# How far ahead of TensorE the order list puts VectorE's and ScalarE's expert slots

## The chip, the core and the metric

The kernel runs on one core of a Trainium2 chip. The metric is the device time of one launch in microseconds (us). TensorE, VectorE, ScalarE, GpSimd (POOL in the rows) and SyncE (SP) each run their own instruction stream and meet through semaphores.

## What is computed

Two layers of a diffusion backbone over 256 context tokens and 256 latent tokens of width 1024, all in float32: attention of two kinds behind one input projection, an output projection, and a feed-forward part that retrieves experts. The last of these is where the change acts:

```python
def peer_ffn(h, p):                       # per block of 128 tokens
    q = (xb @ p['peer_wq']).reshape(128, 8 heads, 2, 128)
    s = einsum('thcd,ckd->thck', q, subkeys);  sv, si = top_k(s, 16)
    cand = all 16 x 16 sums of the two halves;  top_s, pos = top_k(cand, 16)
    eidx = expert number of each;  gate = softmax(top_s)          # 8 x 16 = 128 experts a token
    u, v = peer_u[eidx], peer_v[eidx]                              # rows of 1024 each
    act = gelu(einsum('ted,td->te', u, xb)) * gate
    return einsum('te,ted->td', act, v)
for l in range(2):
    x, xc = x + g1 * attention(x, xc), ...;  x = x + g2 * peer_ffn(norm(x));  (the same for xc in layer 0)
```

Layer 0 has four blocks of 128 tokens in this part (two of context, two latent), layer 1 has two. So there are 6 blocks of 128 expert slots each, 768 slots.

## The kernel before

**A slot** is one expert for each of a block's 128 tokens. GpSimd gathers its u and v rows from HBM into one of eight buffers of EXPERT (L628, 128 partitions x 2048 floats, about 1 MB). VectorE takes the dot product of u with the token (L1524, into DOT; CUSTOM in the trace, ISA in the order's rows). ScalarE makes the Gelu of it (L1107, GEL), times the gate (L1109, WEI), and for three slots of four a diagonal matrix of the weights (L1114, DIAG, three buffers). TensorE multiplies that diagonal by v into two PSUM banks VS (L924, two products that the profile shows as four matmul records). Every fourth slot goes to VectorE instead (L1534, ACC), after the dot of the slot behind it. A buffer of EXPERT comes free when TensorE, or for a fourth slot VectorE, has used it; the gather of the slot eight further on waits for that (L620, L628). ScalarE can write a DIAG buffer only when TensorE has used the one three TensorE slots back.

**The background** is everything else: projections ("in", "up", "out": TensorE L784, L812, weights of 0.25 to 0.5 MB a piece by SyncE), transposes (L716), attention ("attn", one stage a head: scores L852, row maximum on VectorE L1355, exponential on ScalarE L1055, transposes, product with V L860), and the choosing of experts ("pick" and "more", for a second tile of tokens "also" and "then": key queries on TensorE L914, scores L895, top-16 on VectorE L1463 to L1491, then the expert numbers L1496 to L1517).

**Order.** PLAN is one list of stages, made by hand-written rules when the program is built. It lays background stages and slots in one row, mostly one or two slots behind each stage where background is plentiful, four or five where it is not. TensorE and SyncE go through PLAN as it stands. VectorE and ScalarE go through `late(PLAN)`, in which a slot may stand ahead of background that TensorE does first. In the kernel before, of each run of consecutive slots only the first is moved ahead, over the stages directly before it, up to a summed cost of LEAD = 130 (the costs are VectorE's share of a stage by the table COST: 45 for "pick", 40 for "more", 35 for "attn", 40 for an "in" of two tiles). `put_off` says whether a stage may be passed: not a "close", and not the stage that picks the experts of the slot itself or of the next 16. GpSimd gathers in the order of slots.

```python
LEAD = 130                                     # before
while run > 0 and jumped < LEAD and put_off(out[at - 1], first):
    at, run, jumped = at - 1, run - 1, jumped + cost(out[at - 1])
```

Of the kernel before, what the change touches and what calls it, by code (L numbers as in the profile page):

```python
# [30 lines left out]
SLOTS = PH * TOPK  # L31
# [15 lines left out]
AHEAD = 16  # L47
# [18 lines left out]
def blocks_of(l, g):  # L66

    return [4 * l + 2 * g - (2 if l else 0) + t for t in range(2)]
# [83 lines left out]
def mingle(first, second):  # L152
# [4 lines left out]
    for n, s in enumerate(first):  # L157
# [12 lines left out]
COST = {"stat": (45, 0), "norm": (50, 0), "in": (0, 20), "turn": (0, 10), "root": (5, 5), "up": (0, 25), "attn": (35, 0),  # L170
        "hnorm": (20, 0), "heads": (20, 0), "gates": (10, 0), "out": (0, 22), "back": (20, 0), "pick": (45, 0), "more": (40, 0), "also": (45, 0), "then": (40, 0),
        "ada": (18, 0), "adae": (4, 0), "adat": (10, 0), "mod": (5, 0)}
# [3 lines left out]
def cost(s):  # L176
    each, per_tile = COST[s[0]]
    return each + per_tile * (len(s[PER_TILE[s[0]]]) if s[0] in PER_TILE else 0)


def picks_of(stage):

    if stage[0] not in ("more", "then") or stage[3] == 0:
        return []
    _, l, g, h, ts = stage
    return [blocks_of(l, g)[ts[0]] * SLOTS + TOPK * (h - 1)]
# [53 lines left out]
def spans(plan):  # L240

    out = []
    for s in plan:
        if s[0] == "slots" and out and out[-1][0] == "slots" and out[-1][1] == s[1] and out[-1][3] == s[2]:
            out[-1] = ("slots", s[1], out[-1][2], s[3])
        else:
            out.append(s)
    return out
# [41 lines left out]
PLAN = make_plan()  # L290


LEAD = 130


def put_off(stage, slots):

    return stage[0] in COST and not any(at <= slots[1] * SLOTS + slots[3] - 1 + AHEAD for at in picks_of(stage))


def late(plan):

    out, run = [], 0
    for s in plan:
        if s[0] == "slots":
            _, b, q0, q1 = s
            first, at, jumped = ("slots", b, q0, q0 + 1), len(out), 0  # L310
            while run > 0 and jumped < LEAD and put_off(out[at - 1], first):
                at, run, jumped = at - 1, run - 1, jumped + cost(out[at - 1])
            if at == len(out):
                out.append(s)
            else:
                out.insert(at, first)
                out += [("slots", b, q0 + 1, q1)] if q1 > q0 + 1 else []
            run = 0
        else:
            out.append(s)  # L320
            run += 1
    at = {s: n for n, s in enumerate(out)}
    for s in out:
        if s[0] == "slots":
            need = s[1] * SLOTS + (s[3] - 1) // TOPK * TOPK
            assert any(at[p] < at[s] for p in out if need in picks_of(p)), "slots before their pick"
    return out
# [77 lines left out]
def backbone(nc, a, out):  # L405
    ctx = ExitStack()
    with ctx:
# [548 lines left out]
        def _(act):  # L956
# [180 lines left out]
            for stage in late(PLAN):  # L1137
                if stage[0] in do:
                    do[stage[0]](stage)

        @block.vector
        def _(dve):
# [449 lines left out]
            for stage in late(PLAN):  # L1592
                if stage[0] in do:
                    do[stage[0]](stage)
# [43 lines left out]
```

## Time and profile before

| | |
|---|---|
| median of three runs | 2957.7 us (2955.98 to 2963.01) |
| the profiled execution | 2969.66 us, span of its records 2967.8 us |
| busy in the span | TensorE 2190.0, VectorE 1854.1, ScalarE 1148.0, GpSimd 969.0 us |
| mean granted TensorE clock | 0.877 |
| HBM traffic | 973.56 MB read, 328 GB/s over the span |

Slots run from about 259 us to the end, with a break from about 2000 to 2161 us, where layer 0 has none left and layer 1 none chosen yet. Windows of the trace give busy times and the DMA engines' share by stretch; the views of waits say who waited for whom; the timeline shows single instructions. A wait is idle time of an engine that ended with the event named behind the arrow.

### The profile page before, as it was taken

The numbers are of one execution on the slowest core, as the hardware profiler recorded it, in microseconds if no ns is written. First come the engines' busy times: TensorE is split into PE (matmuls) and PEld (weight loads), VectorE is DVE, ScalarE is ACT, GpSimd is POOL, SyncE is SP. The second block draws the span as 40 slices with busy tenths as digits, with TensorE's granted clock in tenths as the row PEclk, the third lists the DMA queues.
The fourth block names the chain that finished last, engine by engine and source line by source line (L and its number), as shares of the span: only waits on it lengthen the run. The fifth ranks groups of instructions, "written<-read, shape, count | busy, mean of one in ns | idle before, by whom it ended". The sixth has DMA issues, their size and how long they took to land.

```text
span 2967.8 us, 26078 instructions
## 1 busy us (share of the span) xinstructions
PE 2190.0 (74%) x6768; PEld 1104.7 (37%) x6768; DVE 1854.1 (62%) x4482; ACT 1148.0 (39%) x3024; POOL 969.0 (33%) x916
## 2 busy tenths in 40 slices
PE   5997677658777787777767877868766777766765
PEld 2544334433433334333323323324533333433322
DVE  0136765874457656888876565543487565777775
ACT  2123463452246725434453243331234454343432
POOL 1012223223223233434443444430033323344553
PEclk9988788879899898888888999988877989889988
DMA  8478879878787698889999999994298969999997
GB/s 296 137 266 312 301 272 347 307 282 333 296 317 252 250 331 328 330 349 398 420 421 372 410 419 416 416 412 145 93 368 318 374 229 356 340 389 416 414 417 309
DMA packets 210714, 976.18 MB, mean 329 GB/s; under 512 B 17533, under 2 KB 70297, under 8 KB 112281
## 3 DMA queue, kind: packets, MB, share of 16 engines
q0 software_dynamic: 123648, 855.69, 73.1%
q1 hardware_dynamic: 86936, 118.99, 11.7%
q8 instruction: 55, 0.90, 0.1%
q14 instruction: 75, 0.61, 0.1%
HBM read 973.56 MB, written 1.05 MB: 328 GB/s over the span
## 4 chain that ended last, share of the span: by engine, by line
PE 40%; DVE 20%; DMA 16%; ACT 15%; issue 7%; POOL 1%; SPq 0%; POOLq 0%; DVEq 0%; ACTq 0%
PE VS L924 19%; DMA EXPERT<-in_peer_uv,FIX 15%; PE PA L784 8%; DVE EXPERT L1524 5%; ACT L1107 3%; PE PB L914 3%; ACT DIAG L1114 2%; DVE SCR L1159 2%; ACT WEI L1109 2%; PE PA L812 2%; PE PB L852 2%; DVE ACC L1534 1%; ACT SCR L1055 1%; ACT GEL L1107 1%; PE VS L742 1%
## 5 line engine op out<-in xcount | busy, mean ns | idle before, releaser
L924 PE MATMUL VS<-EXPERT,DIAG 128*128 128x512 f32 x2304 | 1294.0, 701 | 629.2 <-ACT DIAG L1114 628.3
L628 POOL DMA_INDIRECT EXPERT<-in_peer_uv,FIX x768 | 899.9, 1172 | 1396.4 <-PE VS L924 837.6
L1524 DVE CUSTOM_DVE_ANT_0 EXPERT<-EXPERT,H 128x1024 f32<-128x1024 f32 x768 | 920.8, 1223 | 245.7 <-DMA EXPERT<-in_peer_uv,FIX 234.8
L924 PEld LDWEIGHTS VS<-EXPERT,DIAG 128*128 128x128 f32 x2304 | 469.2, 218 | 1292.2 <-ACT DIAG L1114 835.0
L1107 ACT ACTIVATE GEL<-DOT 128x1 f32<-128x1 f32 x768 | 154.9, 202 | 1093.4 <-DVE DOT L1524 1082.2
L784 PE MATMUL PA<-WT,HT 128*128 128x512 f32 (+2 forms) x768 | 322.9, 567 | 12.2 <-ACT HT L1011 6.0
L1534 DVE SCALAR_TENSOR_TENSOR ACC<-EXPERT,WEI,ACC 128x1024 f32<-128x1024 f32 x192 | 246.2, 1282 | 52.8 <-ACT WEI L1109 52.2
L1114 ACT ACTIVATE DIAG<-IDN,WEI 128x128 f32<-128x128 f32 x576 | 231.2, 401 | 44.8 <-PE VS L924 26.3
L1109 ACT ACTIVATE WEI<-GEL,GATE 128x1 f32<-128x1 f32 x768 | 226.3, 295 | 25.0
L784 PEld LDWEIGHTS PA<-WT,HT 128*128 128x128 f32 x768 | 150.2, 198 | 173.9 <-issue 143.8
L914 PEld LDWEIGHTS PB<-HT,WT 128*128 128x128 f32 x1280 | 188.1, 211 | 33.0 <-issue 26.9
L914 PE MATMUL PB<-HT,WT 128*128 128x128 f32 (+1 forms) x1280 | 198.7, 314 | 1.6 <-issue 1.6
L1107 ACT ACT_TABLE_LOAD x115 | 147.5, 1283 | 6.0
L1355 DVE TENSOR_REDUCE MX<-PB 128x1 f32<-128x512 f32 (+1 forms) x96 | 55.5, 598 | 125.5 <-PE PB L852 125.4
L654 POOL DMA_DIRECT2D EXPERT<-in_w_ada x48 | 34.5, 720 | 292.4 <-PE VS L742 270.5
L620 POOL COPY FIX<-IDX 128x8 uint32 (+1 forms) x96 | 34.4, 359 | 277.7 <-PE VS L924 160.1
L1091 ACT COPY SCR<-PB 128x128 f32<-128x128 f32 (+1 forms) x80 | 22.6, 283 | 195.6 <-PE PB L914 193.6
L1055 ACT ACT_TABLE_LOAD x50 | 64.2, 1283 | 63.2 <-PE PB L852 62.7
L1055 ACT ACTIVATE SCR<-PB,NM 128x512 f32<-128x512 f32 (+1 forms) x96 | 58.7, 614 | 75.1 <-DVE NM L1372 74.3
L1463 DVE MAX8 SV<-PA 128x8 f32<-128x128 f32 x96 | 23.7, 288 | 99.8 <-PE PA L895 99.7
L716 PE MATMUL PB<-IDN,SCR 128*128 128x128 f32 (+1 forms) x374 | 55.3, 294 | 23.9 <-DVE SCR L1159 9.3
L716 PEld LDWEIGHTS PB<-IDN,SCR 128*128 128x128 f32 (+1 forms) x374 | 47.2, 149 | 55.9 <-issue 20.1
(141 smaller groups left out, 1753.8 us busy)
## 6 DMA issues: line engine op xcount, KB each, us to landing
EXPERT<-in_w_ada POOLq DMA_DIRECT2D x48, 1024.0 KB, 11.2
WT<-in_peer_wq SPq DMA_DIRECT2D x80, 512.0 KB
WT<-in_w_in SPq DMA_DIRECT2D x56, 512.0 KB
WT<-in_w_out SPq DMA_DIRECT2D x40, 512.0 KB
EXPERT<-in_peer_uv,FIX POOLq DMA_INDIRECT x768
WT<-in_w_in SPq DMA_DIRECT2D x16, 384.0 KB
WT<-in_w_in SPq DMA_DIRECT2D x20, 288.0 KB
WT<-in_mla_wk_up SPq DMA_DIRECT2D x5, 512.0 KB
```

Source lines behind the costliest of these rows:

```text
L628: pool.indirect_dma_start(out=EXPERT[:, j, :], out_offset=None, in_=a["peer_uv"], in_offset=bass.IndirectOffsetOnAxis(ap=FIX[:, par, j:j + ...
L716: last = nc.tensor.transpose(bank[0:rows, i * P:(i + 1) * P], s, IDN[:, :])
L784: last = nc.tensor.matmul(bank[:, 0:n], HT[:, k, t * P:(t + 1) * P], w[:, k % KP, 0:n], start=(k == 0), stop=(k == KD - 1))
L812: last = nc.tensor.matmul(bank[:, 0:n], HT[:, k0 + k, t * P:(t + 1) * P], w[:, k % KP, 0:n], start=(k == 0), stop=(k == kn - 1))
L914: last = nc.tensor.matmul(bank[:, mine], held["w"][k // HP][:, k % HP, c * P:(c + 1) * P], HT[:, k, mine], start=(k == 0), stop=(k == KD - 1))
L924: ins = nc.tensor.matmul(VSUM[n][:, :], DIAG[:, i, :], EXPERT[:, j, D + n * W:D + (n + 1) * W], start=first, stop=last_one)
L1055: ins = nc.scalar.activation(PR[:, h % 2, c, 0:keys], bank[:, 0:keys], ACT.Exp, bias=NM[:, h % 2, c:c + 1], scale=SC_M if h < MH else SC_D ...
L1107: nc.scalar.activation(GEL[:, one], DOT[:, j:j + 1], ACT.Gelu).then_inc(gelu_ready, 1)
L1109: nc.scalar.activation(WEI[:, one], GEL[:, one], ACT.Copy, scale=gate).then_inc(wei_ready, 1)
L1114: nc.scalar.activation(DIAG[:, i, :], IDN[:, :], ACT.Copy, scale=WEI[:, one]).then_inc(diag_ready, 1)
L1524: nc.vector.tensor_tensor_reduce(out=EXPERT[:, j, 0:D], in0=EXPERT[:, j, 0:D], in1=H2[:, b % HB, :], scale=1.0, scalar=0.0, op0=ALU.mult, ...
L1534: nc.vector.scalar_tensor_tensor(out=ACC[:, :], in0=EXPERT[:, j, D:2 * D], scalar=WEI[:, BY_PE:BY_PE + 1], in1=ACC[:, :], op0=ALU.mult, op ...
```

## The change

Only the list of VectorE and ScalarE changes. TensorE's rows, SyncE's and GpSimd's are the same as before, instruction for instruction; lines move up by one number. Now every slot is moved, not the first of a run alone. A slot passes stages until it meets another slot, a stage that `put_off` keeps, a summed cost of LEAD = 70, or a stage that TensorE reaches more than LEAD_SLOTS = 3 slots earlier. Since slots that were moved leave the stages behind them, the next slot can pass them again.

```diff
-LEAD = 130
-def put_off(stage, slots):
-    return stage[0] in COST and not any(at <= slots[1] * SLOTS + slots[3] - 1 + AHEAD for at in picks_of(stage))
+LEAD = 70
+LEAD_SLOTS = 3
+def put_off(stage, slot):
+    return stage[0] in COST and not any(at <= slot[1] * SLOTS + slot[2] + AHEAD for at in picks_of(stage))
 def late(plan):
-    out, run = [], 0
+    out, before, no = [], {}, 0
     for s in plan:
...
+        if s[0] != "slots":
             out.append(s)
-            run += 1
+            before[s] = no
+            continue
+        for i in range(s[2], s[3]):
+            slot, at, jumped = ("slots", s[1], i, i + 1), len(out), 0
+            while (at > 0 and out[at - 1][0] != "slots" and put_off(out[at - 1], slot) and jumped < LEAD
+                   and no - before[out[at - 1]] <= LEAD_SLOTS):
+                at, jumped = at - 1, jumped + cost(out[at - 1])
+            out.insert(at, slot)
+            no += 1
+    out = spans(out)
```

Counted on the two lists: before, 303 of the 768 slots stand ahead of TensorE's order, nearly all by one stage; now 635 do, 254 by one stage, 316 by two, 65 by three to five. No slot stands later than before.

VectorE while the experts of the second context tile are chosen (head 2): before, between the end of a "pick" (L1491) and the start of its "more" (L1496) stand the dots of slots 73 and 74.

```order
L1491 MAX_INDEX POS<-TS,SCR 128x8
L1524 ISA EXPERT,DOT<-EXPERT,H 128x1024
L1524 ISA DOT 128x1
L1524 ISA EXPERT,DOT<-EXPERT,H 128x1024
L1524 ISA DOT 128x1
L1496 TENSOR_SCALAR AB<-POS 128x16
```

The same place now:

```order
L1490 MAX_INDEX POS<-TS,SCR 128x8
L1523 ISA EXPERT,DOT<-EXPERT,H 128x1024
L1523 ISA DOT 128x1
L1533 SCALAR_TENSOR_TENSOR ACC<-EXPERT,WEI,ACC 128x1024
L1523 ISA EXPERT,DOT<-EXPERT,H 128x1024
L1523 ISA DOT 128x1
L1495 TENSOR_SCALAR AB<-POS 128x16
```

Now these are the dots of slots 76 and 77 (the row into ACC, the fourth-slot product of slot 75, always follows the dot of 76): three slots later ones stand at the same stage.

ScalarE in attention of the first latent tile, between the exponential of the last head with one map and that of the first with two (x2). Before, slots 160 and 161:

```order
L1055 ACTIVATE SCR,SUM<-PB,NM 128x512
L1107 ACT_TABLE_LOAD
L1107 ACTIVATE GEL<-DOT 128x1
L1109 ACTIVATE WEI<-GEL,GATE 128x1
L1114 ACTIVATE DIAG<-IDN,WEI 128x128
L1107 ACTIVATE GEL<-DOT 128x1
L1109 ACTIVATE WEI<-GEL,GATE 128x1
L1114 ACTIVATE DIAG<-IDN,WEI 128x128
L1055 ACT_TABLE_LOAD
L1055 ACTIVATE SCR,SUM<-PB,NM 128x512 x2
```

Now, slots 162 and 163:

```order
L1054 ACTIVATE SCR,SUM<-PB,NM 128x512
L1106 ACT_TABLE_LOAD
L1106 ACTIVATE GEL<-DOT 128x1
L1108 ACTIVATE WEI<-GEL,GATE 128x1
L1113 ACTIVATE DIAG<-IDN,WEI 128x128
L1106 ACTIVATE GEL<-DOT 128x1
L1108 ACTIVATE WEI<-GEL,GATE 128x1
L1054 ACT_TABLE_LOAD
L1054 ACTIVATE SCR,SUM<-PB,NM 128x512 x2
```

Slot 163, a fourth one, has no DIAG. Two slots stand there as before, but two numbers further on. The count of table loads in ScalarE's list is 193 in both programs.

VectorE at the input projection of the latent tiles (the key chunk, whose rotation L1159 waits for the end of TensorE's products). Before, the slot directly ahead of it is 113, followed by 114:

```order
L1524 ISA EXPERT,DOT<-EXPERT,H 128x1024
L1524 ISA DOT 128x1
L1159 TENSOR_TENSOR SCR<-PA,ROPD 128x256 x2
L1159 TENSOR_TENSOR SCR<-PA,ROPD 128x512
L1159 TENSOR_TENSOR SCR<-SCR 128x512
```

Now it is 116:

```order
L1523 ISA EXPERT,DOT<-EXPERT,H 128x1024
L1523 ISA DOT 128x1
L1533 SCALAR_TENSOR_TENSOR ACC<-EXPERT,WEI,ACC 128x1024
L1158 TENSOR_TENSOR SCR<-PA,ROPD 128x256 x2
L1158 TENSOR_TENSOR SCR<-PA,ROPD 128x512
L1158 TENSOR_TENSOR SCR<-SCR 128x512
```

Three more slots are through VectorE when it reaches the rotation. TensorE does slots 113 and 114 behind the products that the rotation waits for.

## Rows read from the trace of the kernel before

**Rows 1.** The page: chain that ended last; the groups of the slot's matmul and dot.

```profile
PE VS L924 19%; DMA EXPERT<-in_peer_uv,FIX 15%; PE PA L784 8%; DVE EXPERT L1524 5%; ACT L1107 3%; PE PB L914 3%; ACT DIAG L1114 2%; DVE SCR L1159 2%; ACT WEI L1109 2%; PE PA L812 2%; PE PB L852 2%; DVE ACC L1534 1%; ACT SCR L1055 1%; ACT GEL L1107 1%; PE VS L742 1%
...
L924 PE MATMUL VS<-EXPERT,DIAG 128*128 128x512 f32 x2304 | 1294.0, 701 | 629.2 <-ACT DIAG L1114 628.3
...
L1524 DVE CUSTOM_DVE_ANT_0 EXPERT<-EXPERT,H 128x1024 f32<-128x1024 f32 x768 | 920.8, 1223 | 245.7 <-DMA EXPERT<-in_peer_uv,FIX 234.8
```

**Rows 2.** Windows: from:to, length, busy time by engine, clock, DMA share, GB/s.

```profile
core 0: us, PE busy (x) PEld busy (x) DVE busy (x) ACT busy (x) POOL busy (x), PEclk, DMA share, GB/s
259.00:1269.00 1010.00, 749.73 (x2334) 393.49 (x2334) 673.95 (x1726) 457.02 (x1099) 305.37 (x290) 0.87 0.83 309
1269.00:2000.00 731.00, 550.18 (x1331) 244.28 (x1332) 497.11 (x1054) 279.35 (x829) 321.03 (x294) 0.90 0.99 403
2161.00:2613.00 452.00, 326.79 (x1003) 165.87 (x1003) 304.59 (x755) 198.69 (x504) 150.44 (x145) 0.86 0.87 334
2613.00:2968.00 355.00, 232.63 (x564) 101.93 (x564) 246.86 (x509) 125.45 (x389) 154.95 (x137) 0.86 0.95 387
503.00:640.00 137.00, 94.00 (x385) 58.27 (x383) 110.07 (x392) 52.62 (x136) 37.09 (x36) 0.83 0.83 314
534.15:550.32 16.17, 11.12 (x48) 7.02 (x48) 13.89 (x50) 6.58 (x17) 5.23 (x5) 0.87 0.83 310
640.00:860.00 220.00, 171.72 (x437) 82.08 (x436) 107.77 (x194) 69.32 (x202) 62.38 (x61) 0.90 0.82 308
860.00:1040.00 180.00, 137.99 (x504) 70.90 (x502) 126.86 (x256) 126.03 (x244) 53.50 (x50) 0.91 0.72 264
```

**Rows 3.** TensorE's waits (total, times, longest), the first four windows in order.

```profile
PE VS L924 <- ACT DIAG L1114: 236.3, 95, 6.8
...
PE VS L924 <- ACT DIAG L1114: 166.9, 87, 5.4
...
PE VS L924 <- ACT DIAG L1114: 120.2, 45, 7.9
...
PE VS L924 <- ACT DIAG L1114: 104.9, 49, 9.4
```

**Rows 4.** The same for windows 503:640 (choosing), 640:860 (projections), 860:1040 (attention).

```profile
PE VS L924 <- ACT DIAG L1114: 42.6, 11, 6.8
...
PE VS L924 <- ACT DIAG L1114: 40.5, 15, 5.2
...
PE VS L924 <- ACT DIAG L1114: 38.9, 24, 5.3
```

**Rows 5.** VectorE's waits: two in 259:1269, one in 860:1040, one in 1269:2000.

```profile
DVE SCR L1159 <- PE PA L784: 75.2, 8, 17.8
...
DVE EXPERT L1524 <- DMA EXPERT<-in_peer_uv,FIX: 2.5, 4, 1.2
...
DVE MX L1355 <- PE PB L852: 40.2, 13, 7.1
...
DVE EXPERT L1524 <- DMA EXPERT<-in_peer_uv,FIX: 142.0, 107, 3.1
```

**Rows 6.** Timeline: start, duration, instruction [idle before it <-releaser].

```profile
529.79 1.88 PE L924 MATMUL VS<-EXPERT,DIAG 128*128 128x512 f32 x4
...
535.28 3.33 PE L924 MATMUL VS<-EXPERT,DIAG 128*128 128x512 f32 x4 [3.61 <-ACT DIAG L1114]
...
541.05 1.28 ACT L1107 ACT_TABLE_LOAD   x1
542.35 0.20 ACT L1107 ACTIVATE GEL<-DOT 128x1 f32<-128x1 f32 x1
...
551.46 3.78 PE L924 MATMUL VS<-EXPERT,DIAG 128*128 128x512 f32 x4 [5.06 <-ACT DIAG L1114]
...
725.62 2.53 PE L924 MATMUL VS<-EXPERT,DIAG 128*128 128x512 f32 x4 [3.58 <-ACT DIAG L1114]
...
914.60 3.68 PE L924 MATMUL VS<-EXPERT,DIAG 128*128 128x512 f32 x4 [4.16 <-ACT DIAG L1114]
```

More of the change, by code:

```diff
@@ L290 @@
 PLAN = make_plan()
-LEAD = 130
-def put_off(stage, slots):
-    return stage[0] in COST and not any(at <= slots[1] * SLOTS + slots[3] - 1 + AHEAD for at in picks_of(stage))
+LEAD = 70
+LEAD_SLOTS = 3
+def put_off(stage, slot):
+    return stage[0] in COST and not any(at <= slot[1] * SLOTS + slot[2] + AHEAD for at in picks_of(stage))
 def late(plan):
-    out, run = [], 0
+    out, before, no = [], {}, 0
     for s in plan:
[L308 to L319, printed above, removed]
-            out.append(s)
-            run += 1
+        if s[0] != "slots":
+            out.append(s)
+            before[s] = no
[8 more added lines that the diff above has]
+    out = spans(out)
     at = {s: n for n, s in enumerate(out)}
```

## The prediction, written before the changed kernel ran

> **What bounds the kernel now.** I read the page first. No engine is full, TensorE being busy 2190 of 2968 us, and one wait stands out: the slot's matmuls waited 628.3 us for the diagonal that ScalarE makes for them, 21% of the span [rows 1]. The chain that ended last runs through these matmuls (19%) and through the gathers (15%) in about equal parts, so the limit changes with the place. The windows say where [rows 2]. From 1269 to 2000 us and from 2613 us to the end the DMA engines' share is 0.99 and 0.95, at 403 and 387 GB/s: 1086 us in which the gathers set the pace. From 259 to 1269 and from 2161 to 2613 us the share is 0.83 and 0.87: 1462 us in which something else does. The waits for DIAG divide into 236.3 + 120.2 = 356.5 us in the second kind and 166.9 + 104.9 = 271.8 us in the first [rows 3], together the 628.3.
>
> In the DMA-bound stretches VectorE stands 142.0 us in 107 waits for gathers that have not landed, from 1269 to 2000 us alone. From 259 to 1269 us it waits so for 2.5 us in all [rows 5]. There the data is in place, and what is late is the dot on VectorE, since a background stage is ahead of it. The timeline shows the pattern [rows 6]: the slot at 529.79 us, first of its run and so moved ahead before, starts without a wait and takes 1.88 us. The slots at 535.28 and 551.46 us wait 3.61 and 5.06 us, each for a dot that VectorE did only after a whole top-16; 725.62 us is the same behind a rotation, 914.60 us the same in attention. Here the wait changes sides: VectorE in its turn waits for TensorE's stages, 75.2 us for projections (L784) from 259 to 1269 us, and 40.2 us for scores in the attention window alone, about what TensorE waits for DIAG there, 38.9 us [rows 4, 5]. Two engines in turn, neither full. That is time a longer lead can overlap.
>
> After a long wait TensorE also runs slower: the four records take 1.88 us where none came before, 3.33 and 3.78 us behind waits of 3.61 and 5.06 us [rows 6], the mark of the 1.2 GHz level against 2.4. The granted clock is 0.83 to 0.91 in the latency-bound windows [rows 2]. A wait that goes gives back up to 1.5 to 1.9 us more.
>
> **The change, part by part.** It adds and removes no instruction. It moves dots (L1524), fourth-slot products (L1534) and ScalarE's GEL, WEI and DIAG ahead of background on their two engines; no DMA is issued there. So the cost side is delay of what is passed, the gain side the waits above. It also lowers LEAD from 130 to 70; since no slot ends up later than before, that costs nothing against the old order.
>
> *Choosing experts, all stretches of it outside the DMA-bound time:* 259 to 365, 503 to 640, 1148 to 1269, 2161 to 2300 and 2510 to 2613 us, 606 us together (borders read off the timeline, an estimate to some us). One head from 534.15 to 550.32 us takes 16.17 us, of which VectorE is busy 13.89 [rows 2]. With any lead a head can't be shorter than that: at most 2.28 us go. The gathers allow it, 0.83 x 16.17 = 13.4 us. VectorE will still wait a little for the scores and for WEI, so I take half, 1.14 of 16.17 us or 7.05%: 606 x 0.0705 = 43 us. Ends: 0, if VectorE meets the same waits elsewhere, and 85.
>
> *Attention,* 365 to 450, 860 to 1040, 2345 to 2440 us, 360 us: in the middle window TensorE waits 38.9 of 180 us for DIAG, with VectorE busy 127, ScalarE 126, TensorE 138 [rows 2, 4]. A stage there needs all three engines one after the other (scores, maximum, exponential, transposes), and the stage that is passed feeds TensorE's next. I take a third of the wait, 13.0 us in 180, so 26 us in 360. Ends: 0 and two thirds, 52.
>
> *Projections and what lies around them,* 450 to 503, 640 to 860, 1040 to 1148, 2440 to 2510 us, 451 us: in 640 to 860 us the wait is 40.5 of 220 us, VectorE is busy only 108 [rows 2, 4]. Again a third, 13.5 in 220, so 451 / 220 x 13.5 = 28 us. There is more idle time on VectorE here, but the DMA share of 0.82 leaves only 0.18 x 220 = 40 us before the gathers and weights fill it, and ScalarE can't be more than three DIAG buffers ahead whatever the list says. Ends: 0 and 55.
>
> All three together, 97 us, lie well under what the DMA engines would allow: 0.17 x 1010 + 0.13 x 452 = 230 us [rows 2].
>
> *The DMA-bound stretches,* 1086 us: four or five slots stand between two stages, and a dot moved ahead starts no earlier than its gather lands. TensorE's 271.8 us of waits stay under other names or the same. I take 0. Ends: a gain of 0.01 x 731 + 0.05 x 355 = 25 us from the share that is left, and a loss of as much: a stage now stands behind up to three dots that each wait 142.0 / 107 = 1.3 us for a landing, which the slots that TensorE does in between (1.88 us each) hide; if that cover were gone in every sixth of about 100 stages there, it would cost 17 times 1.3, or 22 us.
>
> *Late stages elsewhere:* where nothing waits for a landing, a stage is later by the dots that passed it, 1.22 us each [rows 1], while TensorE has one or two slots of 1.88 us to do. I cost this at nothing beyond the halves and thirds taken above.
>
> *A rule on ScalarE's tables.* The rows show a table load of 1.28 us at 541.05 us, and the Gelu behind it starts at 542.35 us, 0.02 us after its end [rows 6]; the count of loads is 193 in either program. The Trainium skill ("ScalarE: Activation LUTs", What ACT_TABLE_LOAD costs) states a drain of about 1.38 us beside each load, some 2.66 us a switch. With that, ScalarE's 126 us in the attention window would be near full and the attention term 0, the time 26 us longer; by the trace the drain isn't there.
>
> **Sum.** 43 + 26 + 28 = 97 us off the profiled execution's 2969.7 us gives 2873. The median of the runs lies 12 us under that execution, so the forecast for the median is **2861 us**.
>
> **Rivals.** *The wait changes its name.* TensorE no longer waits at L924 but at the next stage, for the maximum, transposed copy or key query that is now behind more dots. For it: the two engines hand stages to each other in attention. Against: outside L924 TensorE waits hardly at all now, so there is slack. It would leave a quarter of the gain, 24 us: 2934 us.
>
> *ScalarE binds in attention.* It is busy 126 of 180 us there, and its DIAG now waits for TensorE's slot three back with the exponential queued behind. Then that term is 0: 2887 us.
>
> *Slower: the ring.* Two blocks, 256 slots, take the 1010 us of the first window, so the eight buffers make one trip in 8 x 1010 / 256 = 32 us; the next 256 take 731 us, a trip in 23 us with the queue full. Some 9 us are thus to spare, and dots three slots ahead use up about 3 x 3.9 = 12 us. If VectorE now meets unlanded gathers in the first kind too, it stands there with the stage behind it, and TensorE runs dry. About 230 stages lie in these stretches; at 1.3 us each it decides from 97 / 1.3 = 75 of them, a third. If half are hit, 115 x 1.3 = 150 us are lost against 97 won: 3011 us. Against it: 2.5 us of landing waits now.
>
> *The change does nothing:* the three DIAG buffers and VectorE's own queue keep the real lead where it is. 2958 us.
>
> **Chances.** Forecast 0.60; wait renamed 0.17, of which a tenth ends inside the bound; ScalarE 0.08; ring 0.10; nothing 0.05. A change of 0.3% (9 us) is about what a measurement of this kernel can tell from none. Faster 0.60 + 0.08 + 0.15 = 0.83, within 0.3% 0.07, slower 0.10. The range reaches down to most of the upper ends, about 160 us of the 85 + 52 + 55 = 192: 2795 us, and up past the renamed wait to 2948 us.
>
> **What would show it.** Right: the DIAG wait falls from 356.5 to 200 us or less in the latency-bound stretches, the DMA share there rises to about 0.9, the DMA-bound stretches keep their length within 25 us, and the heads of the choosing take about 15 us. VectorE's 75.2 us at L784 grow shorter or are met by full DIAG buffers. Wrong: new TensorE waits at L860, L716, L784 or L895 of tens of us (renamed wait), landing waits of VectorE far above 2.5 us in the first stretch (ring), or ScalarE near full in attention.

## The result, and the profile after

The changed kernel takes 2759.9 us (2755.77 to 2763.04, four runs) where the kernel before takes 2960.4 us: ratio 0.9322, 95% interval 0.9301 to 0.9343, 200 us less. The forecast was 2861 us with a range of 2795 to 2948. The direction was right, the gain forecast (97 us) was half of the one measured, and the time lies below the range. The two profiled executions, 2969.7 and 2755.8 us, are 214 us apart; readings from the traces add up to that and not to 200.

The page of the changed kernel: span, busy time, chain that ended last, and the groups of slot matmul and dot that answer to [rows 1].

```profile
span 2753.9 us, 26076 instructions
...
PE 2117.5 (77%) x6768; PEld 1091.8 (40%) x6768; DVE 1852.2 (67%) x4482; ACT 1145.8 (42%) x3024; POOL 970.6 (35%) x916
...
DMA EXPERT<-in_peer_uv,FIX 21%; PE VS L923 12%; PE PA L783 9%; DVE EXPERT L1523 7%; DVE ACC L1533 2%; PE PA L811 2%; DVE SCR L1158 2%; PE PB L913 2%; ACT L1106 1%; PE VS L741 1%; ACT L1054 1%; ACT WEI L1108 1%; PE PB L851 1%; ACT HT L1010 1%; ACT DIAG L1113 1%
...
L923 PE MATMUL VS<-EXPERT,DIAG 128*128 128x512 f32 x2304 | 1197.6, 662 | 310.5 <-ACT DIAG L1113 309.6
...
L1523 DVE CUSTOM_DVE_ANT_0 EXPERT<-EXPERT,H 128x1024 f32<-128x1024 f32 x768 | 925.6, 1224 | 353.9 <-DMA EXPERT<-in_peer_uv,FIX 344.1
```

The wait for DIAG is halved, 628.3 to 309.6 us. What the same matmuls are busy fell too, from 1294.0 to 1197.6 us, although there are as many and of the same size. That second number turned out to matter.

Windows of the changed kernel (from:to, length, busy time by engine, clock, DMA share, GB/s). The first four are cut at the dots of slots 0, 256, 512 and 640. The last three hold the same matmuls as 503:640, 640:860 and 860:1040 of [rows 2], to within one record:

```profile
261.00:1124.00 863.00, 702.51 (x2334) 382.74 (x2334) 671.34 (x1725) 455.97 (x1099) 308.62 (x289) 0.92 0.94 361
1124.00:2016.00 892.00, 674.77 (x1903) 328.19 (x1903) 561.19 (x1248) 313.51 (x908) 325.42 (x302) 0.87 0.88 354
2016.00:2414.00 398.00, 307.31 (x1019) 166.23 (x1019) 311.48 (x766) 201.65 (x509) 152.46 (x146) 0.88 0.98 394
2414.00:2754.00 340.00, 230.28 (x548) 99.30 (x548) 240.36 (x499) 121.08 (x384) 153.98 (x135) 0.88 0.95 388
472.00:583.60 111.60, 85.52 (x385) 58.05 (x383) 106.71 (x378) 48.40 (x129) 38.77 (x37) 0.89 0.99 384
583.60:776.10 192.50, 165.60 (x436) 80.71 (x437) 114.17 (x210) 73.90 (x210) 63.92 (x60) 0.92 0.89 344
776.10:923.50 147.40, 130.65 (x505) 70.54 (x504) 122.37 (x252) 124.53 (x239) 55.95 (x51) 0.97 0.88 334
```

The first latency-bound stretch (slots 0 to 256; a stretch where the engines wait for each other and not for gathers) went from 1010 to 863 us, TensorE's busy time in it from 749.7 to 702.5 us and its clock from 0.87 to 0.92. The second, from slot 512 to slot 640, went from 465 us (2161 to 2626) to 398. Slots 256 to 512 with the break behind them took 892 us before (1269 to 2161) and take 892 now; the last stretch 342 and 340. So 147 + 67 us came from the latency-bound stretches, and all the rest is as it was.

What TensorE waits for in the first stretch, then what VectorE does (total, times, longest):

```profile
PE VS L923 <- ACT DIAG L1113: 50.4, 21, 7.1
PE PA L894 <- ACT SCR L1090: 36.8, 11, 4.6
PE PA L859 <- DVE SCR L1368: 12.6, 14, 1.9
...
DVE EXPERT L1523 <- DMA EXPERT<-in_peer_uv,FIX: 37.1, 28, 2.8
DVE SCR L1158 <- PE PA L783: 31.9, 8, 8.1
```

DIAG's 236.3 us [rows 3] are 50.4. Some waiting has other names now, of which the two largest make 49 us, so that TensorE's idle time in the stretch fell by 100 us (260.3 to 160.5) where the wait for DIAG fell by 186. VectorE waits 37.1 us for landings where it waited 2.5 [rows 5]. Both rivals are to be seen; the halved gathers below say what the second cost.

### The profile page after: what moved, and what is told of

Read it like the earlier page. It is cut to its first block, busy times and chain, and to the rows that moved or that the text cites. A ratio compares the mean times of both kernels' runs of the same rounds, so it can differ in the third digit from the quotient of the medians.

```text
span 2753.9 us, 26076 instructions
## 1 busy us (share of the span) xinstructions
PE 2117.5 (77%) x6768; PEld 1091.8 (40%) x6768; DVE 1852.2 (67%) x4482; ACT 1145.8 (42%) x3024; POOL 970.6 (35%) x916
## 4 chain that ended last, share of the span: by engine, by line
PE 33%; DVE 23%; DMA 23%; ACT 12%; issue 7%; POOL 1%; POOLq 0%; SPq 0%; DVEq 0%; ACTq 0%
DMA EXPERT<-in_peer_uv,FIX 21%; PE VS L923 12%; PE PA L783 9%; DVE EXPERT L1523 7%; DVE ACC L1533 2%; PE PA L811 2%; DVE SCR L1158 2%; PE PB L913 2%; ACT L1106 1%; PE VS L741 1%; ACT L1054 1%; ACT WEI L1108 1%; PE PB L851 1%; ACT HT L1010 1%; ACT DIAG L1113 1%
## 5 line engine op out<-in xcount | busy, mean ns | idle before, releaser
L923 PE MATMUL VS<-EXPERT,DIAG 128*128 128x512 f32 x2304 | 1197.6, 662 | 310.5 <-ACT DIAG L1113 309.6
L923 PEld LDWEIGHTS VS<-EXPERT,DIAG 128*128 128x128 f32 x2304 | 462.9, 212 | 912.0 <-issue 469.7
L913 PE MATMUL PB<-HT,WT 128*128 128x128 f32 (+1 forms) x1280 | 204.4, 320 | 15.7 <-issue 15.7
L1106 ACT ACT_TABLE_LOAD x115 | 147.5, 1283 | 6.6 <-ACT SCR L1054 0.8
L715 PE MATMUL PB<-IDN,SCR 128*128 128x128 f32 (+1 forms) x374 | 55.9, 295 | 73.2 <-DVE SCR L1307 21.5
L715 PEld LDWEIGHTS PB<-IDN,SCR 128*128 128x128 f32 (+1 forms) x374 | 45.1, 145 | 104.6 <-ACT SCR L999 26.3
L894 PE MATMUL PA<-SKT,SCR 128*128 128x128 f32 x192 | 38.4, 342 | 60.0 <-ACT SCR L1090 60.0
L811 PE MATMUL PA<-WT,HT 128*128 128x512 f32 (+1 forms) x136 | 65.9, 636 | 17.5 <-ACT HT L1042 10.1
L894 PEld LDWEIGHTS PA<-SKT,SCR 128*128 128x128 f32 x192 | 33.0, 239 | 84.7 <-ACT SCR L1090 75.1
```

The source lines that it names most:

```text
L715: last = nc.tensor.transpose(bank[0:rows, i * P:(i + 1) * P], s, IDN[:, :])
L811: last = nc.tensor.matmul(bank[:, 0:n], HT[:, k0 + k, t * P:(t + 1) * P], w[:, k % KP, 0:n], start=(k == 0), stop=(k == kn - 1))
L913: last = nc.tensor.matmul(bank[:, mine], held["w"][k // HP][:, k % HP, c * P:(c + 1) * P], HT[:, k, mine], start=(k == 0), stop=(k == KD - 1))
L923: ins = nc.tensor.matmul(VSUM[n][:, :], DIAG[:, i, :], EXPERT[:, j, D + n * W:D + (n + 1) * W], start=first, stop=last_one)
L1106: nc.scalar.activation(GEL[:, one], DOT[:, j:j + 1], ACT.Gelu).then_inc(gelu_ready, 1)
```

## The experiments

### One stage, or several?

`one_stage` lets every slot pass one stage and no more; `pair` does so only for the first two slots behind a stage; `slots1` and `slots2` narrow the distance (how many slots earlier TensorE may reach the stage) and keep LEAD = 70; `lead130` lets a slot pass more stages.

```diff
 one_stage:  LEAD = 1,   LEAD_SLOTS = 3
 pair:       LEAD = 1,   LEAD_SLOTS = 1
 slots1:     LEAD = 70,  LEAD_SLOTS = 1
 slots2:     LEAD = 70,  LEAD_SLOTS = 2
 lead130:    LEAD = 130, LEAD_SLOTS = 3
```

> The new rule with LEAD = 1: every slot may pass exactly one stage, never two; 635 of 768 slots stand one stage ahead (before: 303, after: 635, of which 381 by two or more). Theory A (the wait sits at the second slot of each run of two, which the old rule left behind its stage; passing that one stage ends it): at least two thirds of the 200 us come, 2825 us or less. Theory B (one stage of VectorE's work, up to 5 us of top-16, is longer than one slot of TensorE, so the second stage of lead is needed): less than half comes, 2860 to 2930 us.

> LEAD = 1 and LEAD_SLOTS = 1: only the first two slots behind a stage stand ahead of it, by that one stage. Against the old rule, 206 slots are moved, all of them second slots but a few, each by one stage, and some first slots lose a second stage. Theory A (second slots): this smallest edit brings 170 us or more, 2790 us or less. Rival (a standing lead that carries over from stage to stage is needed): 2830 us or more.

> LEAD_SLOTS = 1 instead of 3, LEAD 70 kept: a slot may pass a stage only if TensorE reaches it at most one slot earlier; 509 slots ahead instead of 635. Theory A (second slots): most of the gain, near 2800 us, since second slots still pass their stage. Theory B (depth): well under half, 2870 to 2930 us.

> LEAD_SLOTS = 2: 579 slots ahead. Theory A: within 15 us of the changed kernel (2760). Theory B: a clear step between one and three, 2790 to 2830 us.

> The new rule with LEAD = 130 instead of 70: 121 slots pass three stages and 219 two (70: 34 and 316). If the latency-bound stretches are now full by the gathers (DMA share 0.94 and 0.98 there), nothing is left to win: 2750 to 2765 us. If depth still pays, 2740 or less. If stages that are passed too far make TensorE wait (the renamed wait), 2775 us or more.

| kernel | us | ratio to before (95%) |
|---|---|---|
| pair | 2760.2 | 0.9318 (0.9288 to 0.9347) |
| one_stage | 2761.8 | 0.9321 (0.9306 to 0.9337) |
| slots1 | 2759.1 | 0.9324 (0.9298 to 0.9350) |
| slots2 | 2746.0 | 0.9271 (0.9256 to 0.9287) |
| the change | 2759.9 | 0.9322 (0.9301 to 0.9343) |
| lead130 | 2779.0 | 0.9370 (0.9343 to 0.9397) |

Theory A holds and B falls. `pair` moves 206 slots more than the old rule, by one stage, and brings the whole 200 us. Counted on the two lists, all 206 are second slots of their run. The depth beyond one stage adds nothing to the total. The old rule moved the first slot of each run, and in a run of two the second stayed behind the stage, so TensorE met the full length of VectorE's stage once a run. [rows 6] shows the pair: the slot at 529.79 us without a wait, the next, at 535.28 us, with 3.61.

By stretch the depth is not nothing. Slots 0 to 256 in `pair`:

```profile
258.00:1139.00 881.00, 704.59 (x2336) 380.25 (x2334) 672.64 (x1726) 456.68 (x1099) 303.26 (x290) 0.92 0.93 354
```

One stage brings 129 of the 147 us there, and the change 18 us more. It loses them further on: from slot 256 to 512 `pair` takes 881 us and the change 892, from 512 to 640 they take 395 and 398. These are single profiled executions, and `slots2` and `slots2_warm` (below), which have the same program from slot 256 to 512, differ by 6 us there. So the 18 us look real, and where they are lost is less sure.

More depth still even costs: every run of `lead130` is slower than every run of the change, by 19 us in the median. Three of TensorE's waits over the whole of `lead130` (total, times, longest):

```profile
PE VS L923 <- ACT DIAG L1113: 306.7, 142, 9.4
PE PA L894 <- ACT SCR L1090: 59.6, 22, 6.3
...
PE PB L715 <- DVE SCR L1307: 23.8, 6, 8.0
```

and over the whole of `one_stage`:

```profile
PE VS L923 <- ACT DIAG L1113: 463.5, 251, 9.4
PE PA L799 <- DVE GD L1158: 27.8, 14, 3.4
...
PE PA L894 <- ACT SCR L1090: 14.2, 8, 3.8
```

One stage of lead leaves 157 us more of DIAG waits than `lead130` has, and is 17 us faster. Part of what the deep leads no longer wait for DIAG they wait at L894 and L715: the renamed wait of the forecast is real. A total of one named wait is no measure of the kernel. But it does not explain why `lead130` is slower than the change, which waits as long at L894 over the whole:

```profile
PE PA L894 <- ACT SCR L1090: 60.0, 23, 4.6
```

The 19 us are lost between slots 0 and 256 (882.5 us against 863.2). There TensorE's waits for DIAG and at L894 and L859 add up to 94 us in `lead130` and 100 us in the change, and VectorE's wait for landings grew from 37.1 us to this:

```profile
DVE EXPERT L1523 <- DMA EXPERT<-in_peer_uv,FIX: 54.5, 35, 5.4
```

That speaks for the ring rather than for the renamed wait; no run separates the two. LEAD_SLOTS = 2 is the best of the six, 14 us under the change in the median, with an interval clear of the change's.

### Where

The new rule for blocks 0, 1 and 4 alone (`new_where_late`), or for 2, 3 and 5 alone (`new_where_dma`), the other slots by the old rule:

```diff
+        slow = s[1] in (0, 1, 4)
+        if not slow:          # new_where_dma: if slow
+            (the old rule: the first slot of the run, LEAD = 130)
+            continue
         for i in range(s[2], s[3]):
```

> The new rule for the slots of blocks 0, 1 and 4 alone (the latency-bound stretches); the slots of blocks 2, 3 and 5 stand as before. Theory: all of the gain is made there and the rest is bound by the gathers, so 2755 to 2770 us. Rival (the gain is also in the DMA-bound stretches, or is paid for there): 2790 us or more, or under 2745.

> The opposite: the new rule for blocks 2, 3 and 5 alone. Theory: no change, 2950 to 2970 us (before: 2960). Rival: 20 us or more off it either way.

Measured: 2753.6 us, ratio 0.9297 (0.9263 to 0.9330), a little under the 2755 to 2770 expected, and 2966.7 us, ratio 1.0021 (1.0008 to 1.0034). All of the gain is made in the latency-bound blocks. In the gather-bound ones the new order is worth nothing and may cost 0.2%. `slots2_late` put the two best readings together:

> LEAD_SLOTS = 2 and only for the latency-bound blocks 0, 1 and 4, the rest as before: the two best readings put together. If both were real: 2735 to 2750 us, under the changed kernel's 2760 by 10 or more. If they were noise between placements: 2745 to 2765.

2750.3 us, ratio 0.9272 (0.9246 to 0.9299): no better than `slots2`, and a time that both expectations allow. Differences below 10 us are not resolved.

### Do the gathers bound it now?

The DMA share in the shortened stretches is 0.94 to 0.98. Both kernels were run with gathers of half the bytes, from a table of the u rows alone. The v half of each buffer keeps what was there, so these kernels leave the experts' v rows out of the result; two runs each:

```diff
-    out=EXPERT[:, j, :], ... in_=a["peer_uv"]
+    out=EXPERT[:, j, 0:D], ... in_=a["peer_uv"]       # u rows alone
```

> The kernel before, with gathers of the u rows alone (half the bytes; the v half of each buffer keeps what was there, so the weighted sums are left without their experts' values). Theory C (in the old order the latency-bound 1462 us are set by VectorE and TensorE in turn, not by the gathers): they keep 95% of their length, and only the 1086 DMA-bound us shrink, to what the engines need. Rival: everywhere shorter in the same proportion.

> The same halved gathers in the changed kernel. Theory D (with the change the gathers have become the bound of the former latency-bound stretches too, DMA share 0.94 and 0.98): those two, 863 and 387 us long, get at least 8% shorter, so that the change is worth more here than 200 us. Rival E (they are bound by VectorE and TensorE and the high DMA share is only a company): they shorten by under 3%.

Windows of `half_before`, slots 0 to 256, and of `half_after`, slots 0 to 256 and 512 to 640:

```profile
261.00:1270.00 1009.00, 748.62 (x2334) 392.38 (x2334) 672.91 (x1725) 457.02 (x1099) 305.34 (x289) 0.87 0.55 173
```

```profile
256.00:1115.00 859.00, 703.78 (x2334) 385.15 (x2334) 669.63 (x1725) 454.81 (x1099) 310.76 (x289) 0.92 0.63 204
1882.00:2257.00 375.00, 299.86 (x1022) 161.19 (x1021) 309.98 (x767) 201.29 (x509) 154.35 (x147) 0.91 0.70 231
```

`half_before` takes 2803.1 us and keeps 1009 us in the first stretch: theory C holds. `half_after` takes 2524.1 us, but its first stretch keeps 859 of 863 us at a DMA share of 0.63, and the second 375 of 398. Theory D falls for the first: a share of 0.94 was company and no bound, and its landing waits of 37.1 us, the mark of the ring rival, cost it no more than those 4 us. The second, at 0.98, got 6% shorter, between what the two theories had said: there some 23 us hang on the bytes gathered, and VectorE's landing waits of 37.9 us fall to 5.3. Cut at the same matmuls in both traces, it is the choosing of experts that gets shorter (524 to 495 us over both stretches); projections keep their 387 and 386 us and attention its 293 and 297. What the halving saves otherwise is in the DMA-bound blocks.

### The clock that a wait takes with it

TensorE's books: before, the span of 2967.8 us was 2190.0 busy and 777.8 idle; after, 2117.5 busy and 636.4 idle. Of 214 us, 141 are idle time and 73 are busy time of the same work at a higher clock. To price the second part without touching the order, small matmuls of a zero block were put ahead of slots, in the kernel before: twelve ahead of each of 92 second slots in `warm`, whether they waited or not, eight ahead of slots that had waited 2.4 us or more in the others. They add zeros to the slot sum. The edit of the others:

```diff
+    if kind == "one" and slot_no(b, v0) in WARM_AT:
+        for n in range(WARM):
+            nc.tensor.matmul(VSUM[0][0:32, 0:P], ZERO[:, :], IDN[:, :], start=False, stop=False)
```

> The kernel before, with 12 matmuls of a zero block (32 columns of zeros times the 128-wide identity, added into the slot sum, about 1.5 us in all) ahead of the wait of 92 second slots in blocks 0, 1 and 4. Nothing of the order changes; TensorE is merely busy in a part of its wait. Theory (a wait costs its own length and then a stretch of matmuls at 1.2 GHz, and this second part is what the sum left out): the slot matmuls' busy time falls by 40 us or more, the time by 20 to 60 us. Rival (the clock plays no part): busy time of the slots unchanged, time the same or up to 30 us longer.

> The kernel before, with 8 of the zero matmuls (1.2 to 1.9 us by the 263 us that 1104 of them took in the run warm) ahead of the 65 slots that waited 2.4 us or more in the latency-bound stretches, 254.9 us together; so they should fit inside the waits and cost nothing themselves. Those slots' matmuls took 3.4 us each on the mean, 1.5 more than at 2.4 GHz. Theory (the clock after a wait is itself on the path): up to 65 x 1.5 = 98 us of slot time come back and 30 to 90 us of the total, 2870 to 2930 us. Rival (a slot's own matmuls after a wait are not what the next stage waits for, the gain comes from the order alone): slot time falls, the total stays within 10 us of 2960.

> The kernel before, with the same 8 zero matmuls ahead of the 48 slots that waited 2.4 us or more in the DMA-bound stretches (168.5 us of waits, their matmuls 3.1 us each on the mean, so up to 60 us of slot time to be had). Theory (there the gathers set the pace, and neither order nor clock of TensorE matters): total within 9 us of 2961. Rival (the clock is on the path everywhere): 20 to 40 us less.

`warm` gave 2965.9 us, ratio 1.0008 (0.9995 to 1.0020), with the slots' busy time 66 us down, to 1228.3: the busy time fell as its theory expected, the time did not. Taken alone it says that the clock is not on the path. But its 1104 zero matmuls took 263.2 us, 2.9 us for each slot instead of the 1.5 expected, and in the trace of before 49 of the 92 slots had waited less than that, 27 of them less than 1 us. So it is inconclusive.

`warm_long`, with eight zero matmuls (128.5 us in 65 places, 2.0 us each) where the wait is 2.4 us or more, gave 2904.9 us, ratio 0.9810 (0.9794 to 0.9827): 57 us less with no instruction of the old order moved. Its slot group with the waits:

```profile
L927 PE MATMUL VS<-EXPERT,DIAG 128*128 128x512 f32 x2304 | 1234.9, 673 | 518.4 <-ACT DIAG L1120 518.1
```

The slots' busy time is 59 us down, nearly all of it at the 65 slots (220.8 to 162.1 us), and the total 57. The wait for DIAG is 110 us shorter because the zero matmuls fill it. The first stretch is 979 us instead of 1010 (dot of slot 0 at 259.3 us, of slot 256 at 1238.2). `warm_dma` took 42 us off the slots' busy time in the gather-bound blocks, to 1252.5, and 4 us off the total: 2957.3 us, ratio 0.9988 (0.9977 to 1.0000). So the clock is on the path where TensorE and VectorE hand work to each other, and off it where gathers set the pace.

Does it come on top of the new order?

> The new rule with LEAD_SLOTS = 2 and the 8 zero matmuls ahead of the 11 latency-bound slots that still wait 2.4 us or more there (50.9 us, matmuls of 3.7 us on the mean). Theory (the new order has already collected the clock's share, since its waits are gone): at most 11 x 1.8 = 20 us less than slots2, 2726 to 2746 us. Rival (clock and order are separate gains, so that the 57 us of warm_long come on top): 2700 us or less.

2744.8 us, ratio 0.9264 (0.9247 to 0.9281), against 2746.0 for `slots2`. Hardly anything comes on top: the waits that it would have to fill are gone. The eleven slots that were left took 40.2 us in `slots2` and take 31.3, so 9 us were to be had, too little to be told from none in the total.

## Why the forecast was wrong

**Where the gain lies: right.** The division into latency-bound and DMA-bound stretches, 0 for the latter, held to 2 us, and `new_where_dma` confirms it. So did the reading of the slots in [rows 6] as two engines in turn. That the gathers leave room for the gain held for the first stretch; in the second, at a DMA share of 0.98, halving them gave back some 23 us. Of the 230 us that the forecast said the DMA engines would allow, 214 were used.

**The three terms: each mis-sized, by the same two steps.** Since TensorE's list is the same, both traces can be cut at the same matmuls, those at the borders that the forecast used, and each row below is the same work. Idle and busy are TensorE's, in us, each figure rounded by itself:

| | before | after | gain | from idle | from busy | in the sum (upper end) |
|---|---|---|---|---|---|---|
| choosing experts | 605 | 524 | 81 | 47 | 35 | 43 (85) |
| attention | 363 | 293 | 71 | 56 | 15 | 26 (52) |
| projections | 447 | 387 | 61 | 41 | 20 | 28 (55) |
| together | 1416 | 1203 | 212 | 143 | 69 | 97 (192) |

The first step that failed is "I take half" and "I take a third". Nothing in the trace supported a half or a third; it was caution put into a term. In the middle window of choosing VectorE is now busy 106.7 of 111.6 us, 96%, and seven heads in a row take 13.4 us each where they took 16.5: VectorE's own busy time became the bound there, as the ceiling of 13.89 in 16.17 us had said, and the discount below that ceiling was wrong. In attention the wait for DIAG went from 38.9 us [rows 4] to this, in 776.1 to 923.5 us:

```profile
PE VS L923 <- ACT DIAG L1113: 1.0, 3, 0.3
```

with new waits of TensorE of 8.6 us at L859 the largest. Against 87.9 us of DIAG waits in all attention before, TensorE's idle time fell by 56, two thirds and not one; against 86.5 us in projections by 41, about half. Had the shares been right, the idle part alone would have been 143 us instead of 97.

The second step is the clock. The forecast noted that "A wait that goes gives back up to 1.5 to 1.9 us more" and then left it out of the sum, and out of the bounds. It is the 69 us of the column "from busy": the same matmuls in less time, in attention 138.0 us before and 130.9 now, at a clock of 0.97 in that window instead of 0.91 [rows 2]. It alone takes projections past their upper end; attention had passed its own by idle time, and choosing stayed inside. `warm_long` prices the clock at 57 us by itself (it did not reach every slot: 21 of the 65 still took over 3 us, where 55 had, and the one at 539.82 us took 3.78 us after 3.19 us more of waiting). With 97 + 69 = 166 us the forecast would have been 2792 us; the shares make the other 46 us.

```profile
534.70 1.93 PE L936 MATMUL VS<-IDN,ZERO 128*32 128x128 f32 x16
539.82 3.78 PE L927 MATMUL VS<-EXPERT,DIAG 128*128 128x512 f32 x4 [3.19 <-ACT DIAG L1120]
```

**The range.** Its lower end took "most of the upper ends" of terms whose ends lacked the clock. The sum of those ends, 192 us, is still 8 short of what came.

**What the forecast said of the change.** It treated the longer lead as the cause. `pair` shows that the second slot of each run was, and that one stage is enough for the total. The count of moved slots by depth, which stood in front of it, could have been set against the waits: 316 slots at two stages looked like the substance and were not.

**The rivals.** The renamed wait is there in part, about 49 us at L894 and L859 in the first stretch, and the gains in the table are net of it. The ring came as landing waits of 37.1 us, which cost 4 us at most in the first stretch, and of 37.9 us in the second, where halved gathers gave back some 23. ScalarE in attention, busy 124.5 of 147.4 us, is now close to binding, but did not hold the gain up. As to the table loads, there are 50 in that window (25, 24 and 1), each 1283 ns; over the whole the traces have 240 in either kernel, not the 193 of the forecast. The drain of 1.38 us a load that the Trainium skill states ("ScalarE: Activation LUTs", What ACT_TABLE_LOAD costs) would be 69 us more, and 23 us are idle: the trace disagrees, no such time is there. Nor was there before, where it would have made ScalarE's 126 us in 180 not "near full" but 195.

**The signs named ahead.** DIAG wait in the latency-bound stretches 200 us or less: it is 50.4 and 23.5. DMA share about 0.9: 0.94 and 0.98. DMA-bound stretches within 25 us: within 2. Heads of about 15 us: 13.4. VectorE's 75.2 us at L784: 31.9. But signs of being wrong came with them: TensorE's 36.8 us at L894 are tens of us where the renamed wait was to show, and landing waits went far above 2.5 us. Both are marks of a cost, and neither says how large it is; only the runs did.

What stays open: what separates `slots2` from the change by 14 us. By their traces it is 6 us longer from slot 0 to 256 and 7 us shorter from 512 to 640, where its TensorE clock is 0.91 instead of 0.88, and no run isolates that. Open too is what costs `lead130` its 19 us, and how far the idle and the busy part are separate gains, since a wait and its clock end together.

## What to carry to other kernels

When two in-order engines hand work to each other, look at which item of each run still stands behind the other's stage; moving that one item by one stage can bring all that a deep reordering does, and depth beyond it can win in one stretch and lose as much in another. Price a TensorE wait as its own length plus the slow matmuls behind it, and put both into the sum and its bounds: here the second part was a third of the whole, 69 of 212 us. A high DMA share is not yet a bound; halve the bytes and see whether the stretch gets shorter. And cut two traces at the same instructions before comparing their stretches.

## What was not expected of the hardware

Zero matmuls of 2.0 us, put ahead of waits of 2.4 us and more, shortened a kernel by 57 us without doing any of its work, while the granted clock from 259 to 1269 us rose from 0.87 to 0.93. Twelve of them, 2.9 us, ahead of 92 slots of which 49 had waited less (`warm`), gave nothing. And a stretch at a DMA share of 0.94 lost 4 of 863 us when its gathers were halved.
